# Feed-forward output products of a two-block transformer: one 512-column and one 256-column product per weight tile in place of three of 256 columns

## The reference, cut to what matters

```
x = layer_norm(ALPHA * x + gate * (square(relu(h @ w_ff_in)) @ w_ff_out))       # first block, once

def swiglu_ffn(h, w_in, w_out):                                                 # four times
    g, u = jnp.split(h @ w_in, 2, axis=-1)
    return (jax.nn.silu(g) * u) @ w_out
x = x + 0.5 * swiglu_ffn(rms_norm(x, norm), w_in, w_out)
```

## Time and profile before

| | us |
|---|---|
| median of 3 runs | 1606.15 |
| lowest and highest run | 1599.41, 1606.45 |
| span of the profiled execution (first to last instruction) | 1602.3 |
| PE busy | 1548.0 (97%) |
| DVE busy | 1067.1 (67%) |
| ACT busy | 835.1 (52%) |
| mean granted TensorE clock | 0.993 of full speed |

### The profile page before, as it was taken

One profiled execution on the slowest core, in us unless ns is written; L12 is line 12 of the kernel. 1 busy time (PEld: TensorE's weight loads), 2 busy tenths in 40 slices (PEclk: granted clock), 3 DMA queues, 4 the chain that ended last, 5 costly groups with the idle time before them and its releaser, 6 DMA issues.

```text
span 1602.3 us, 31666 instructions
## 1 busy us (share of the span) xinstructions
PE 1548.0 (97%) x12977; PEld 1515.4 (95%) x12977; DVE 1067.1 (67%) x1557; ACT 835.1 (52%) x1210; POOL 171.2 (11%) x223
## 2 busy tenths in 40 slices
PE   6999999999999999999999999999999999999998
PEld 6899989999998999999999999999998889999998
DVE  7887877886656666575666557665656676566653
ACT  6566546755545444564544454444465555454442
POOL 2013200400113500010100000000100111000000
PEclk9999999999999999999999999999999999999999
DMA  9653963465553554562454565555653014355553
GB/s 381 262 198 107 350 253 132 158 244 185 201 191 115 210 200 164 189 231 96 175 205 176 173 207 197 193 169 185 234 192 132 27 65 173 106 181 187 182 174 116
DMA packets 45126, 293.14 MB, mean 183 GB/s; under 512 B 5201, under 2 KB 6497, under 8 KB 15713
## 3 DMA queue, kind: packets, MB, share of 16 engines
q1 hardware_dynamic: 41184, 265.49, 46.4%
q0 software_dynamic: 3840, 26.23, 4.2%
HBM read 288.02 MB, written 3.67 MB: 182 GB/s over the span
## 4 chain that ended last, share of the span: by engine, by line
PE 77%; DVE 11%; ACT 6%; DMA 4%; issue 2%; DVEq 0%; POOL 0%; SPq 0%; ACTq 0%
PE G L449 23%; PE G L451 22%; PE G L450 22%; DVE w_lo L1636 4%; ACT w_hi L1087 3%; PE O L668 3%; PE L L1048 1%; PE T L654 1%; DMA mod_x<-w_ada 1%; DMA raw<-w_xv 1%; PE L L917 1%; DVE X L1762 1%; DMA raw<-w_wouta 1%; ACT x_hi L1170 1%; DMA raw<-w_f1in 1%
## 5 line engine op out<-in xcount | busy, mean ns | idle before, releaser
L1636 DVE TENSOR_TENSOR w_lo<-raw,w_hi 128x2048 fp32r<-128x2048 f32 (+1 forms) x256 | 541.4, 2118 | 262.8 <-ACT w_hi L1087 262.2
L449 PE MATMUL G<-x_hi,w_hi 128*128 128x256 f32 (+1 forms) x2183 | 611.9, 280 | 12.6 <-DVE w_lo L1636 7.9
L450 PE MATMUL G<-x_lo,w_hi 128*128 128x256 f32 (+1 forms) x2183 | 607.0, 278 | 0.0
L451 PE MATMUL G<-x_hi,w_lo 128*128 128x256 f32 (+1 forms) x2183 | 606.9, 278 | 0.0
L1087 ACT ACTIVATE w_hi<-raw 128x2048 fp32r<-128x2048 f32 (+1 forms) x260 | 458.9, 1768 | 150.1 <-DMA raw<-w_ffout 35.3
L449 PEld LDWEIGHTS G<-x_hi,w_hi 128*128 128x128 f32 (+1 forms) x2183 | 412.0, 189 | 18.9 <-DVE w_lo L1636 9.5
L450 PEld LDWEIGHTS G<-x_lo,w_hi 128*128 128x128 f32 (+1 forms) x2183 | 412.2, 189 | 0.1
L451 PEld LDWEIGHTS G<-x_hi,w_lo 128*128 128x128 f32 (+1 forms) x2183 | 411.8, 189 | 0.1
L449 PE MATMUL G<-hid_hi,w_hi 128*128 128x256 f32 x1280 | 360.7, 282 | 2.9 <-DVE hid_lo L1668 2.3
L451 PE MATMUL G<-hid_hi,w_lo 128*128 128x256 f32 x1280 | 356.7, 279 | 0.0
L450 PE MATMUL G<-hid_lo,w_hi 128*128 128x256 f32 x1280 | 356.6, 279 | 0.0
(11 more groups left out here) (420 smaller groups left out, 1873.3 us busy)
## 6 DMA issues: line engine op xcount, KB each, us to landing
raw<-w_f1in SPq DMA_DIRECT2D x44, 1024.0 KB, 4.8
raw<-w_f2in SPq DMA_DIRECT2D x44, 1024.0 KB, 4.7
raw<-w_f1out SPq DMA_DIRECT2D x32, 704.0 KB, 4.1
raw<-w_f2out SPq DMA_DIRECT2D x32, 704.0 KB, 4.0
raw<-w_ffin SPq DMA_DIRECT2D x16, 1024.0 KB, 4.8
raw<-w_ffout SPq DMA_DIRECT2D x16, 1024.0 KB, 4.8
mod_x<-w_ada POOLq DMA_DIRECT2D x12, 1024.0 KB, 8.5
mod_w<-w_ada POOLq DMA_DIRECT2D x8, 1024.0 KB, 12.0
```

Source lines behind the costliest of these rows:

```text
L449: mm(out, l_hi, r_hi, start=start, stop=False)
L450: mm(out, l_hi, r_lo, start=False, stop=False)
L451: return mm(out, l_lo, r_hi, start=False, stop=stop)
L1636: v.tensor_tensor(w_lo[b][:, 0:s.size], raw[b][:, 0:s.size], w_hi[b][:, 0:s.size].bitcast(F32), ALU.subtract).then_inc(s_lo, 1)
```

## The change

The high and low halves of a hidden chunk now lie directly behind one another in `hid_two` (128 x 512 per chunk). A new helper `gemm_wide` takes the place of `gemm_a` in `ffn_out`: per unit one matmul of the high weight tile over all 512 columns, into the whole bank, and one of the low weight tile over the 256 high columns, into the first half. The bank then holds high-by-high plus low-by-high in its first half, high-by-low in its second, and DVE adds both halves to X, in two instructions with a wait for itself between them. `hid_hi` and `hid_lo` remain for the other stages that used them, with 16 chunks each.

```diff
-        hid_hi = place("hid_hi", [P, 32, S], F32R, 0)
-        hid_lo = place("hid_lo", [P, 32, S], F32R, 32)
+        hid_hi = place("hid_hi", [P, 16, S], F32R, 0)
+        hid_lo = place("hid_lo", [P, 16, S], F32R, 32)
+        hid_two = place("hid_two", [P, 32, 2 * S], F32R, 0)
+        unit_hi, unit_lo = hid_two[:, :, 0:S], hid_two[:, :, S:2 * S]
...
+            def gemm_wide(s, slot, j, x_two, kn, k0, start, stop, i=0, between=None):
+                n = s.n0 + slot
+                slot_begins(s, slot, j if start else None, i, 2)
+                wh = w_hi[n % RING][:, 0:kn * P].rearrange("p (k c) -> p k c", k=kn)
+                wl = w_lo[n % RING][:, 0:kn * P].rearrange("p (k c) -> p k c", k=kn)
+                for k in range(kn):
+                    if between and k == 1:
+                        between()
+                    mm(G[j % 2][:, :], wh[:, k, :], x_two[:, k0 + k, :], start=start and k == 0, stop=False)
+                    last = mm(G[j % 2][:, 0:S], wl[:, k, :], x_two[:, k0 + k, 0:S], start=False,
+                              stop=stop and k == kn - 1)
+                last.then_inc(s_mm, 1)
...
-                        gemm_a(s, 2 * g + part, s.j0 + g, hid_hi, hid_lo, kn=kn, nf=1, k0=part * kn,
-                               start=part == 0, stop=part == 1, i=i, groups=2)
+                        gemm_wide(s, 2 * g + part, s.j0 + g, hid_two, kn, part * kn, part == 0, part == 1, i)
...
-                    act_(hid_hi[:, bass.ds(c0, chunks), :], hb[slot % 2][:, 0:width].rearrange("p (k c) -> p k c", k=chunks),
+                    act_(unit_hi[:, bass.ds(c0, chunks), :], hb[slot % 2][:, 0:width].rearrange("p (k c) -> p k c", k=chunks),
...
+                if nf == 1:
+                    own(v.scalar_tensor_tensor(X[:, g, :], G[j % 2][:, S:2 * S], mod1[:, gate0 + g:gate0 + g + 1],
+                                               X[:, g, :], ALU.mult, ALU.add))
...
+                    if nf == 1:
+                        own(v.scalar_tensor_tensor(X[:, g, :], G[j % 2][:, S:2 * S], factor, X[:, g, :],
+                                                   ALU.mult, ALU.add))
...
-                    v.tensor_tensor(hid_lo[:, bass.ds(c0, chunks), :],
+                    v.tensor_tensor(unit_lo[:, bass.ds(c0, chunks), :],
                                     hb[slot % 2][:, 0:width].rearrange("p (k c) -> p k c", k=chunks),
-                                    hid_hi[:, bass.ds(c0, chunks), :].bitcast(F32), ALU.subtract)\
+                                    unit_hi[:, bass.ds(c0, chunks), :].bitcast(F32), ALU.subtract)\
                         .then_inc(q(s.name + ".lo"), 1)
```

## The result

| | before | changed |
|---|---|---|
| median, us | 1606.15 (7 runs, 1598.87 to 1607.82) | 1613.21 (7 runs, 1606.94 to 1618.98) |
| span of the profiled execution | 1602.3 | 1616.2 (its own time 1617.96) |

The ratio of changed to before is 1.0064, with a 95% interval of 1.0039 to 1.0088: slower by 6 to 14 us, 10 us in the middle. The forecast was 1596.5 in a range of 1587 to 1606.5. The result lies outside it, on the other side of no change.

What follows compares the result with a forecast made beforehand. PE, busy for 97% of the span, was taken as the bound: 10.9 us saved on products, less 0.94 and 0.47 for evictions, gave -9.5 us, from 1606.15 to 1596.6, called 1596.5; range 1587 to 1606.5.

Steps and rivals of the forecast that it cites:

- It is a fixed price per product: Output stages: each product costs 6.7 ns over its columns whatever its width, so a unit takes 333.3 ns.
- the overhead goes with the columns: nothing is gained: Bound for output-stage units: a 512-column product costs twice 113.3 ns, so dropping one product saves nothing.
- the weight load as the price: Rival, chance 0.26: in output stages the weight load sets the spacing, unit 329 ns, median 1592.5 us.
- A steady beat of equal products and loads, which a 512-column product breaks: f2out0 and f2out1: their 117.8 ns spacing is such a beat, so they go to the 113.3 ns spacing's price.
- The 7.0 us booked for the f2out stages: Saving forecast in f2out0 and f2out1: 352 units at 20.0 ns each.
- the 3.9 us of the near stages: Saving forecast in ffout, f1out1 and seven tiles of f1out0, all at 113.3 ns spacing: 586 units at 6.7 ns.
- the far spacing stays or spreads: Rival, chance 0.16: f2out0 and f2out1 stay at 117.8 ns spacing, 1599.7; or all five output stages take 342.2 ns, 1605.
- It does not do what it says: Rival, chance 0.10: the 512-column product costs as two of 256, only the evictions are left, 1607.5 us.
- The rival on the slower side: Rival, chance 0.05: four input stages after output stages lose the 113.3 ns spacing, 17.8 us, giving 1614.5.
- f2out1 0.47: End of f2out1: the added eviction stands alone on the path to the end and costs 0.47 us.
- f1out0 0.94: End of f1out0: the added evictions of tiles 6 and 7 each cost 0.47 us, 0.94 together.
- Behind ffout "free": After ffout: the added eviction is hidden in the norm's 2.32 us wait for ACT's root and costs nothing.

Runs made afterwards that it cites:

- e9: Changed kernel, f1out1 and f2out1 operands read as bfloat16 four bytes apart, two equal products per unit: 226.7 ns for 512 columns, 113.4 for 256.
- e11: Changed kernel, hidden pair stored as packed bfloat16, weights read as upper two bytes, product widths varied by stage: 216.0 ns for 512 columns.
- e2: Changed kernel with the 512-column product issued as two of 256, both evictions kept: median 1603.31 against 1600.42 for the kernel before, ratio 1.0023.
- e4: Changed kernel with one product cut once near the start of four output stages, ffout left alone: one run, 1611.82 us.
- e10: Kernel before with one 256-column product cut into 128+128 near the start of ten stages: median 1603.13 against 1606.09, ratio 0.9975.
- e12: Kernel before with one 256-column product cut into 128+128 in the four f1out and f2out stages and xo: median 1607.58 against 1605.34, ratio 1.0010.
- e1: Kernel before with only the new placing of the hidden halves, products and eviction as before: median 1598.52 against 1600.42, ratio 0.9984.
- e5: Kernel before with one 256-column product cut into 128+128 in f2out0, f1out1 and f2out1: median 1601.80 against 1604.48, ratio 0.9981.
- e8: Changed kernel without the second scalar_tensor_tensor of each eviction: median 1612.27 against 1604.48 for the kernel before, ratio 1.0041.
- e3: Changed kernel with the hidden halves back at their old places, 32 KiB apart, the 512-column product reading two pieces: one run, 1611.22 us.

## Why the prediction was wrong, point by point

- **"It is a fixed price per product."** This is the step that failed. I read 6.7 or 11.1 ns over 256 columns as a toll per instruction. It is a price per column: over 512 columns it is 22 ns (235 - 213.3), over 256 it is 11. Units cost 353.3 ns and not 333.3. By two-byte elements (e9, e11) about half of it comes from the distance of the moving elements; what the rest is stays open. The bound "the overhead goes with the columns: nothing is gained" was in the list, but I worked it at the near spacing, as 340 ns, where the changed product can only run at the far one. The true value lay beyond the bound that I had drawn.
- **The evidence for it** was thin and I could have seen it. The earlier trace rows are read to 10 ns, as much as the whole effect., 60-column weights at 0.35 us for three, spoke against the weight load as the price; I took it as support for the only other reading that I had kept. The earlier trace rows were the best rows: plain float32 takes 0.430 us for 512 columns, two clocks of 2.4 GHz for each, with 2 to 3 ns over, and e11 has the same 2.5 ns over with packed two-byte elements. Both fit a price that hangs on how fast the elements are read and not on the instruction; for plain float32 no run tested it.
- **"A steady beat of equal products and loads, which a 512-column product breaks."** There is such a beat and the 512-column product breaks it, but it is the other one. I took the far spacing for the beat and the near one for the free course; no stage with wide products ran near (23 of 23), and with the same products in equal pieces of 256 columns four stages of five did (e2). The 7.0 us booked for the f2out stages were 0, and the 3.9 us of the near stages became a loss of 7.7.
- **The rival "the far spacing stays or spreads"** had the right name, 0.16, and the wrong price: all stages at 342.2 ns was taken from the fixed toll. At 353.3 its sum would have been 586 x 13.3 + 1.4 = 9.2 us slower. **"It does not do what it says"** had the right price of the product and the wrong base. **The rival on the slower side** was somewhere else altogether: the input stages kept their near spacing behind the new rhythm. That they go far at times was seen only later (e4, e9, e10, e11, e12), once or twice per trace.
- **Evictions.** Hidden in mid-stage: right, DVE has 40 instructions more and PE never waits for `w_lo` within a stage. f2out1 0.47: right, 0.53 measured in the tails. f1out0 0.94: right for the chain (0.90), but behind PE's longer wait the clock fell, 1.5 us more, which the forecast did not have; in e2 and e9, with the same wait, it did not fall. Behind ffout "free": 0.7 us between the two traces, but from ffout's last product to f1out0's first it is 137.7 to 138.4 us in e1, e5, e8, e10 and before with one eviction (e12, whose f1in0 ran far, left out) and 137.5 to 138.8 in e2, e3, e4, e9 and the changed kernel with two, so no cost shows. The sum of 1.4 us stands beside 0 to 7 us by e2.
- **Writes, weight slots, DMA:** nothing moved, as said; e1 shows it by itself.

## What to carry to other kernels

Before a product is made wider to save instructions, find out whether its overhead is per instruction or per column, by a run of the wide form alone; two spacings of one narrow form can't tell. A float32r stream costs more than one clock of 2.4 GHz per column here (233 ns for 512 columns, where packed bfloat16 takes 216), in part because its moving elements lie four bytes apart; equal products of 256 columns at 113.3 ns were the cheapest form of it. And an eviction that doubles on a path where PE waits can cost more than its own length: 0.9 us behind f1out0, and 1.5 more in the traces where the clock fell behind the longer wait.

## What the runs showed of the hardware that I had not expected

- Packed two-byte elements: 216.0 ns for 512 columns. The same elements four bytes apart: 226.7. float32r: 233 in runs of equal products, 235 beside 256-column ones.
- Equal float32r products of 256 columns run at 113.3 or 117.8 ns, and a stage keeps the one that it falls into. f1out0 up to its cut is the same program in e5, e10, e12 and before: near before and in e5, far in e10 and e12.
- A product cut in two of 128 columns moved all eight far hidden stages to near, and ffin in the seven traces where it came far; xq stayed far, two of two.
- Behind f1out0 a wait of PE of 1.56 us was followed by 3.4 us at 1.2 GHz in five traces of seven, with wide products or without; e2 and e9, with the same wait, stayed at full clock there, and so did all six traces with a wait of 1.0 to 1.1 us.
